# A hybrid pooling and windowed-attention layer on eight cores: another order of the loads and first projections in the opening

## The reference, cut to what matters

```python
# x (16, 4096, 1024), ctx (16, 256, 1024), one layer
shift, scale, gate = adaln(c, w_mod, b_mod)          # silu(c) @ w_mod + b_mod, three blocks of 1024
h_ctx = modulate(rms_norm(ctx, g_pre), c_shift, c_scale)
k_ctx, v_ctx = h_ctx @ w_in[:, K], h_ctx @ w_in[:, V]
h = modulate(rms_norm(x, g_pre), shift, scale)
xa, ga, q, k, v, gb, gm = split_columns(h @ w_in)    # 512, 512, 1024, 256, 256, 1024, 2048
y_a = pool_mixer(xa, pool_w, pool_scale) * silu(ga)
y_b = windowed_attention(rope(q), rope(k), v, k_ctx, v_ctx, sink) * silu(gb)
        # 16 heads, keys of block i-1, i, i+1 (128 each) and 256 context keys; exp(sink) joins the sum
g = sigmoid(gm)
merged = g[:, :1024] * (y_a @ w_branch_a) + g[:, 1024:] * (y_b @ w_branch_b)
out = x + gate * rms_norm(merged @ w_out, g_post)
```

## Time and profile before

| | us |
|---|---|
| median of 2 runs | 2343.43 (2341.91 to 2344.96) |
| the profiled execution | 2342.27 |
| its span on the slowest core (0) | 2340.7 |
| spans of the eight cores | 2330.9 to 2340.7 |
| PE busy, of the span | 2215.8 (95%) |
| first steady step starts at about | 262 |

### The profile page before, as it was taken

How to read it: one execution, slowest core, us unless ns; L and a number is a source line. 1 busy time by engine, 2 the same in 40 slices (tenths; PEclk the granted TensorE clock), 3 DMA queues, 4 the chain that set the end, 5 groups by cost and what they waited for, 6 DMA issues and landing times.

```text
span 2340.7 us, 50018 instructions; the slowest of 8 cores (2330.9 to 2340.7 us)
## 1 busy us (share of the span) xinstructions
PE 2215.8 (95%) x16101; PEld 1030.9 (44%) x16392; DVE 1281.3 (55%) x3176; ACT 1185.6 (51%) x2291; POOL 870.5 (37%) x1074
## 2 busy tenths in 40 slices
PE   7478899999999999999999999999999999999997
PEld 2234344444444444444444444444444444444443
DVE  1225556555565655556566645656565565656542
ACT  2235554546555455545545465555556555554531
POOL 1212434343342434334343433434343433434333
PEclk9779999999999999999999999999999999999999
DMA  8975855655555564645556475545546554544353
GB/s 233 246 99 92 154 153 154 166 146 155 164 137 147 157 166 134 164 150 142 149 162 177 140 172 163 138 141 153 161 140 163 162 149 137 162 136 145 100 184 127
DMA packets 209171, 358.12 MB, mean 153 GB/s; under 512 B 131884, under 2 KB 134060, under 8 KB 206520
## 3 DMA queue, kind: packets, MB, share of 16 engines
q1 hardware_dynamic: 206024, 335.97, 49.9%
q0 software_dynamic: 2896, 18.94, 5.9%
HBM read 310.09 MB, written 45.10 MB: 152 GB/s over the span
## 4 chain that ended last, share of the span: by engine, by line
PE 82%; DVE 6%; DMA 5%; issue 4%; ACT 1%; POOL 1%; SPq 0%; DVEq 0%; ACTq 0%; POOLq 0%
PE pb L589 35%; PE pb L968 9%; PE pb L720 9%; PE pb L890 8%; PE pb L781 7%; PE pb L807 6%; PE pb L881 4%; PE pb L645 2%; DVE s_yb L825 2%; DMA s_xt<-x 1%; DVE s_scr L606 1%; DMA s_ropet<-rope 1%; PE pb L356 1%; DMA s_ws<-wg_scr 1%; DVE s_Ga L713 1%
## 5 line engine op out<-in xcount | busy, mean ns | idle before, releaser
L784 ACT ACTIVATE s_PT<-pb 128x512 bf16<-128x512 f32 x1264 | 652.1, 605 | 214.0 <-PE pb L781 214.0
L589 PE MATMUL pb<-s_hT,s_ws 128*128 128x512 bf16 x2665 | 645.3, 382 | 13.8 <-DMA s_ws<-wg_scr 3.0
L589 PEld LDWEIGHTS pb<-s_hT,s_ws 128*128 128x128 bf16 x2784 | 262.0, 98 | 341.1 <-issue 52.9
L922 POOL TENSOR_TENSOR s_mgT<-s_scr 128x512 bf16<-128x512 f32 x128 | 163.4, 1277 | 585.7 <-DVE s_scr L861 580.2
L589 PE MATMUL pb<-s_hT,s_W 128*128 128x512 bf16 x1502 | 346.7, 382 | 3.7 <-issue 2.3
L861 DVE SCALAR_TENSOR_TENSOR s_scr<-s_Tm,pb 128x512 f32<-128x512 bf16 x256 | 175.4, 685 | 294.0 <-PE pb L890 121.2
L856 ACT ACTIVATE s_Tm<-pb 128x512 bf16<-128x512 f32 x256 | 154.8, 605 | 263.0 <-PE pb L589 211.7
L606 DVE TENSOR_TENSOR s_scr<-pb,s_ropet 128x512 f32<-128x512 f32 x320 | 204.1, 685 | 138.2 <-PE pb L589 91.8
L720 PE MATMUL pb<-s_W,s_hT 128*128 128x512 bf16 x1003 | 241.4, 381 | 1.3 <-issue 0.3
L968 PE MATMUL pb<-s_ws,s_mgT 128*128 128x512 bf16 x956 | 231.1, 381 | 6.7 <-DMA s_ws<-wg_scr 1.5
L589 PEld LDWEIGHTS pb<-s_hT,s_W 128*128 128x128 bf16 x1536 | 144.7, 98 | 197.2 <-issue 36.6
(11 more groups left out here) (138 smaller groups left out, 2239.5 us busy)
## 6 DMA issues: line engine op xcount, KB each, us to landing
s_ws<-wg_scr SPq DMA_DIRECT2D x344, 512.0 KB, 4.5
s_xr<-x SPq DMA_DIRECT2D x63, 512.0 KB, 4.7
y<-s_xr SPq DMA_DIRECT2D x60, 512.0 KB, 5.0
s_xt<-x SPq DMA_DIRECT2D x58, 512.0 KB, 4.7
wg_scr<-w_g POOLq DMA_DIRECT2D x22, 512.0 KB, 12.6
s_ropet<-rope SPq DMA_DIRECT2D x16, 512.0 KB, 4.5
s_ws<-w_mod SPq DMA_DIRECT2D x5, 1024.0 KB, 13.3
s_W<-w_in POOLq DMA_DIRECT2D x4, 1024.0 KB, 22.7
```

The source lines that it names most:

```text
L589: E("pe", lambda e, k=k, rhs=rhs: e.matmul(out=pb[:, :], lhsT=lhs(k), rhs=rhs, start=(k == 0), stop=(k == 7)), reads=hb + wbufs(k), writes ...
L784: E("act", lambda e, g=g: e.activation(out=PT[:, jb, g, :], in_=banks[g][0][:, :], func=AF.Exp, scale=0.125), reads=[banks[g][1]], writes= ...
L922: E("pool", lambda e: e.tensor_tensor(out=mgT[:, c, :], in0=u[0][:], in1=v[0][:], op=ALU.add), reads=[u[1], v[1]], writes=[bf(f"mgT{c}")])
```

## The change

It does six things. The six loads of ctx and x are issued without waiting for W2 and W3. The order behind them becomes rope, `w_mod` blocks 4 and 5, then `sink`, the next tile, the `g_rows`. Five of the 22 `gcast` are issued by POOL at once behind the weight casts, before the first projection, and the other 17 from 16.0 on at 3.6 (before: all 22 from 28.0 at 3.8); the first four `gload` go from 62 to 74. On PE the context's norms and transposes come before the values, only one of the four `q_unit` of group 0 stands before the woven part, `ctx_kv(0)` comes behind the transposes of tiles 4 to 7, then three `q_unit`, and `esink` (ACT), the values of group 1, `gate_rows(4)`, keys of group 1, `gate_rows(5)`; attention starts at 19.5 of the planned clock, not 12.5. In the later part of the opening the `xa`, `ga`, `ctx_kv(1)`, `q_unit` and pooling steps change places, and `pool_flush(3)` follows `pool_next(3)` at once. The PE transposes of tiles 0 to 3 are put out 4.5 later than their `pvs` and that of tile 63 3.0 later; `pvs` moves from 0.83 and 0.91 of a tile's width to 0.85 and 0.92 in every tile.

```diff
-                    later(3.0, P(turn_yb, t)) if 4 <= t < TT - 1 else turn_yb(t)
+                    later(3.0 if t >= 4 else 4.5, P(turn_yb, t))
-            ... (0.83, 1.2, P(pvs, 0)), (0.91, 1.2, P(pvs, 2))]
+            ... (0.85, 1.2, P(pvs, 0)), (0.92, 1.2, P(pvs, 2))]
...
-        for n in range(2):
-            next_load([bf("W2")])
-        ld(sinkb, sink_d.partition_broadcast(128), "sinkb", [bf("sinkb")])
+        for n in range(6):
+            next_load()
         load_rope(0)
-        for n in range(4):
-            next_load([bf("W3")])
         load_wmod(4)
         load_wmod(5)
+        ld(sinkb, sink_d.partition_broadcast(128), "sinkb", [bf("sinkb")])
+        if BPC > 1:
+            next_load()
         for j in range(2):
             ...grow loads
-        if BPC > 1:
-            next_load()
         ld(view(edge, 0, [[1, 64]]), edge_d, "edge", [bf("edge")])
         mod_quad(0, act=(1, 4, 7))
+        casts = list(range(14)) + [20, 14, 15, 16, 17, 21, 18, 19]
...
-        E("act", lambda e: e.activation(out=esink[:], in_=sinkb, func=AF.Exp), ...)
-        k_unit(0)
-        v_unit(0, 0)
-        v_unit(0, 1)
+        for i in range(5):
+            gcast(casts.pop(0))
         norm_sum()
         norm_sum()
         xs = [norm_scale(), norm_scale()]
-        q_unit(0, 0)
-        turn_pe_ctx(xs[0], 0, "dve")
-        q_unit(0, 1)
-        turn_pe_ctx(xs[1], 1, "act")
         norm_sum()
         norm_sum()
+        k_unit(0)
+        for j in range(2):
+            turn_pe_ctx(xs[j], j, "act")
+        xs = [norm_scale(), norm_scale()]
         mod_ctx()
-        xs = [norm_scale()]
-        q_unit(0, 2)
-        xs.append(norm_scale())
         norm_sum()
-        q_unit(0, 3)
         norm_sum()
-        load_rope(1)
-        xs.append(norm_scale())
-        xs.append(norm_scale())
+        v_unit(0, 0)
+        v_unit(0, 1)
+        xs += [norm_scale(), norm_scale()]
+        q_unit(0, 0)
...
+        first = [(0.45, P(front_turn, i, 4 + i, 0, ("dve", "act")[i % 2])) for i in range(4)]
+        if BPC > 1:
+            first += [z(next_load)]
+        first += [(3.5, P(ctx_kv, 0)), z(mod_quad, 1, range(8), (1, 4, 7))]
+        first += [(3.46, P(q_unit, 0, r)) for r in range(1, 4)] + [z(load_rope, 1), z(esink_exp)]
+        first += [(1.75, P(v_unit, 1, 0)), (1.75, P(v_unit, 1, 1)), (7.0, P(gate_rows, 4)), (3.46, P(k_unit, 1)), (7.0, P(gate_rows, 5)), z(load_gg, 0)]
...
+        first += [(1.73, P(ga_unit, 0, c)) for c in range(4)] + [z(pool_part, 0, 6.0)]
...
+        first += [(3.46, P(q_unit, 1, 3)), z(pool_next, 3, 5.0), z(pool_flush, 3)]
         first += [(1.73, P(ga_unit, 1, c)) for c in range(4)]
         for n, g in enumerate(casts):
-            later(28.0 + 3.8 * n, P(gcast, g))
+            later(16.0 + 3.6 * n, P(gcast, g))
         for n in range(2, NSL):
-            later(62.0 + 3.8 * n, P(gload, n))
-        run(first, range(4), 12.5)
+            later(74.0 + 3.8 * n, P(gload, n))
+        run(first, range(4), 19.5)
```

More of the change, by code:

```diff
@@ L1034, in pvs @@
                 if g0:
-                    later(3.0, P(turn_yb, t)) if 4 <= t < TT - 1 else turn_yb(t)
+                    later(3.0 if t >= 4 else 4.5, P(turn_yb, t))
             fr = [0.02, 0.18, 0.34, 0.50, 0.66] if nb == 5 else [0.02, 0.20, 0.40, 0.60]
             s = [(f, 0.75, P(vis, jb)) for jb, f in enumerate(fr)]
-            s += [(0.10, 1.73, P(gb, t, 0)), (0.26, 1.73, P(gb, t, 1)), (0.83, 1.2, P(pvs, 0)), (0.91, 1.2, P(pvs, 2))]
+            s += [(0.10, 1.73, P(gb, t, 0)), (0.26, 1.73, P(gb, t, 1)), (0.85, 1.2, P(pvs, 0)), (0.92, 1.2, P(pvs, 2))]
             s.sort(key=lambda v: v[0])
@@ L1217, in build_program @@
             cast(ws[:, i, :], wg_d[18 + i], [bf(f"ws{i}")])
-        E("act", lambda e: e.activation(out=esink[:], in_=sinkb, func=AF.Exp), reads=[bf("sinkb")], writes=[bf("esink")])
-        k_unit(0)
-        v_unit(0, 0)
-        v_unit(0, 1)
+        for i in range(5):
+            gcast(casts.pop(0))
         norm_sum()
@@ L1248, in front_turn, with esink_exp @@
             (turn_pe_ctx if ctx else turn_pe_lat)(xs[n], j, eng)
-        first = [(3.5, P(ctx_kv, 0))] + [(0.45, P(front_turn, i, 4 + i, 0, ("dve", "act")[i % 2])) for i in range(4)]
-        first += [z(mod_quad, 1, range(8), (1, 4, 7)), (3.46, P(k_unit, 1)), (1.75, P(v_unit, 1, 0)), (1.75, P(v_unit, 1, 1))]
+        def esink_exp():
+            E("act", lambda e: e.activation(out=esink[:], in_=sinkb, func=AF.Exp), reads=[bf("sinkb")], writes=[bf("esink")])
+        first = [(0.45, P(front_turn, i, 4 + i, 0, ("dve", "act")[i % 2])) for i in range(4)]
@@ L1252, in build_program @@
         if BPC > 1:
-            first += [z(next_load), z(front_norm), z(front_norm)]
-        first += [(7.0, P(gate_rows, 4))]
+            first += [z(next_load)]
+        first += [(3.5, P(ctx_kv, 0)), z(mod_quad, 1, range(8), (1, 4, 7))]
+        first += [(3.46, P(q_unit, 0, r)) for r in range(1, 4)] + [z(load_rope, 1), z(esink_exp)]
+        first += [(1.75, P(v_unit, 1, 0)), (1.75, P(v_unit, 1, 1)), (7.0, P(gate_rows, 4)), (3.46, P(k_unit, 1)), (7.0, P(gate_rows, 5)), z(load_gg, 0)]
+        first += [z(next_load)] if BPC == 1 else [z(front_norm), z(front_norm)]
@@ L1255, in build_program @@
+        first += [(0.25, P(fold_unit, k)) for k in range(8)]
+        first += [(1.73, P(xa_unit, 0, c)) for c in range(4)]
         if BPC > 1:
-            first += [(0.45, P(front_turn, 4 + j, j, 1, "act")) for j in range(2)] + [z(mod_ctx)]
-        first += [(7.0, P(gate_rows, 5)), z(load_gg, 0)]
+            first += [(0.45, P(front_turn, 4 + j, j, 1, "act")) for j in range(2)] + [z(mod_ctx), z(next_load)]
+        first += [(1.73, P(xa_unit, 1, c)) for c in range(4)]
+        first += [(1.73, P(ga_unit, 0, c)) for c in range(4)] + [z(pool_part, 0, 6.0)]
@@ L1258, in build_program @@
         if BPC > 1:
             first += [(3.5, P(ctx_kv, 1))]
[L1260 to L1265, removed]
@@ L1266, in build_program @@
-        first += [(3.46, P(q_unit, 1, 3)), z(pool_flush, 3)]
+        first += [(3.46, P(q_unit, 1, 0)), z(pool_next, 1, 6.0), (3.46, P(q_unit, 1, 1)), (3.46, P(q_unit, 1, 2)), z(pool_next, 2, 5.0)]
+        first += [(3.46, P(q_unit, 1, 3)), z(pool_next, 3, 5.0), z(pool_flush, 3)]
         first += [(1.73, P(ga_unit, 1, c)) for c in range(4)]
-        casts = list(range(14)) + [20, 14, 15, 16, 17, 21, 18, 19]
         for n, g in enumerate(casts):
-            later(28.0 + 3.8 * n, P(gcast, g))
+            later(16.0 + 3.6 * n, P(gcast, g))
```

## The result

The changed kernel takes 2378.4 us (median of two runs, 2377.3 and 2379.4) against 2343.4: 1.0149 times the time before [1.0105, 1.0193], 1.5% slower. The forecast was 2346 with a range up to 2364, so it was wrong: the change was forecast to cost next to nothing and costs 35 us. Some executions of every kernel here ran several per cent longer at a lower clock on one die or both; all ratios are of the others. The profiled run took 2377.3; its slowest core is core 5 (2375.8 us), where it was core 0 before (2340.7).

The account below looks back on a forecast made before the run. PE was busy 95% of the span; the opening's stretch was bound by a 512 KB load (rope) and an 8 KB one (sink). 2342.3 + 15 (sink stall) - 11 (later transposes, clock) = 2346.3, left at 2346; range 2316 to 2364.

Parts of the forecast that it names:

- Step (1), loads without waits: Opening: six tile loads fit the gap before the casts and beside the key weights; costs nothing, at worst 4 us.
- Step (2): Opening: rope issued about 55.3, ctx's norms freed, gate_rows(4) ending near 106, not 147.8; order wins about 40 us.
- Step (3), the sink: Opening: sink waits behind w_mod 4 and 5 and ten gcasts of 4.0 us; lands about 149 (138 or 157).
- small pieces travel together: Rival, 22%: eight 1 KB pieces count as one packet, sink passes before the gcasts, rope(1) is late; 2325 us.
- Step (4), from the sink to gate_rows(5): ACT waits for the sink, PE idles 107 to about 152, gate_rows(5) ends about 172; +15 us (+3 to +22).
- Steps (5) to (8), the second half: Later transposes, moved pvs, remaining gcasts with later gloads, and pool order; together -11 us.
- Nothing is given back: Rival, 21%: in the second half DVE, not the yb wait, limits PE, so the 11 us fall away; 2359 us.
- Steps (5) and (6): Later transposes of tiles 0 to 3: -9 us and -2 for clock (-13 to 0); moved pvs: 0 (-3 to +3).
- steps (7) and (8): Second half: twelve gcasts remaining with later gloads, 0; pool_flush(3) straight behind pool_next(3), 0, up to +4 us.
- The last transpose: Tile 63's later transpose: a wait of the same kind, 1 us, taken at nothing.
- No blockade: Rival, 7%: gcasts do not hold back the loads; gate_rows(5) ends near 125, 32 us early; 2299 us.
- The slower side: Rival, 21%: DVE limits PE in the second half and the 11 us fall away; 2359, or 2368 with 4.8 us gcasts.

Follow-up runs that it names:

- both: Changed kernel with sink, g_rows and edge loads issued ahead of rope and all gcasts back at the earlier kernel's times; ratio to before 0.9936 [0.9901, 0.9971].
- five gcasts alone: Kernel before, with only five gcasts issued straight behind the weight casts, the other 17 from 28.0 on; ratio to before 1.0068 [1.0039, 1.0097].
- loads alone: Kernel before, with only the six loads of ctx and x no longer waiting for W2 and W3; ratio to before 0.9921 [0.9891, 0.9950].
- no yb: Changed kernel with the transposes and pvs put back as before the change; two runs, 2381.6 and 2397.0 us.

## Why the prediction was wrong, step by step

The mechanism was the one forecast: a sink behind w_mod 5 and the gcasts, ACT standing for it, PE out of banks in vis(1). The direction and the class (within 2%, which I gave 94%) came out too; the size did not. On the slowest core 35.1 us were lost where I had 4, and the 31.1 between them lie in three places: 11.4 up to the end of gate_rows(5), 10.9 in the second half and 8.8 after it. In the mean of the cores, which the accident of one core moves less, it is 8.8, 16.2 and 1.4, and 4.6 for a slowest core further from the mean.

**Step (1), loads without waits: right.** The keys start at 58.45 behind hT's landing, 2.4 us later than the earlier trace rows; priced 0 to 4. Alone, the step is worth 13.8 us at gate_rows(5).

**Step (2): right.** DVE had rope by 69.09 (forecast 68.5), and PE ran until 100. But gate_rows(4), which I had put ahead of vis(1) and finished by about 107, stood behind it.

**Step (3), the sink: right in kind, 8.9 us short.** One packet of each queue in turn, also for pieces of 1 KB: 1018 to 1012 packets from 62 to 105 us, with 5.85 MB against 3.07, and 230 to 230 from 110 to 145. That refutes the rival *small pieces travel together*, and with it the rule of the Trainium skill ("DMA: Bandwidth & Descriptors", Queues, rings and completion order) of 9 to 17 descriptors a packet, as far as it goes for these loads. What was short is the price of a gcast. Ten of them went ahead of the sink, as forecast. Their 160 packets of 32 KB began at 98.7 us (I had 103) and were over at 153.2 (I had 145); the sink came 4.7 us behind them (I had 4). So ten gcasts took 54.5 us where I had 41.5: the packets alone 45.6, 4.56 a gcast and not 4.0, q1's packets between them 6.0 where I had 1.5, and 2.9 that I can't place. My upper bound of 157 used 4.8; the sink came at 157.9.

The 4.0 was a mean over two prices.'s own stretch in two parts, q0 of core 0 before the change, 130 to 150 us and 150 to 180:

```profile
q0 software_dynamic: 144, 2.62, 78.1%
q0 software_dynamic: 194, 3.15, 95.3%
```

That is 3.1 us a gcast and then 4.8, with 19 packets of q1 in all: it was not for want of the other queue that the first were cheap. In 130 to 140 four of the eight cores had gcasts in flight, from 150 on all eight, and after the change all eight from 102 on. That the gcasts of the other cores set the price fits the traces of five kernels (before, after, both, five gcasts alone, loads alone): some 3 us a packet where few cores copy or all copy with pauses, some 4.7 where all copy without a pause. No run tests it by an edit.

**Step (4), from the sink to gate_rows(5): forecast +15, measured +26.4** (183.7 on core 5 against 157.3) and 23.8 in the mean of the cores. Of the 11.4, 8.9 are the sink's. The other 2.5 (with 0.3 from rounding of my 172) are work: I let 23 us pass between the sink and the end, 15 of products, with margins for ACT and the clock; it was 25.8, as gate_rows(4) stood behind the stall with 9.55 us (7.38 before), while PE began 0.9 us behind the sink and not 3. (The margins that I named, 3 and 3, make 21 with the 15 of products; 2 us of my 23 have no term.)

**Steps (5) to (8), the second half: in the mean of the cores this is the term that failed by most.** Forecast -11, measured +5.2 (-0.1 on the slowest core). By its sum it is the case that I called *Nothing is given back*, at a higher price; by its parts it is not. Steps (5) and (6) held: the transposes with the moved `pvs` gave 8.2 us in the changed kernel (13.4 in the kernel before). What failed is what I put at nothing in steps (7) and (8), or did not price at all: the other order of the second half, with a first half that ends in a stall. It cost 13.4 (107.9 to 121.3, "no yb"), and 13.4 less 8.2 is the 5.2. Of the 13.4, 10.8 are idle time of PE (14.1 to 24.9) and 2.5 busy time, at a granted clock of 0.87 where it was 0.92. The idle time stands ahead of two lines: 8.5 us ahead of L807 (0.8 before) and 3.3 ahead of L428 (0.9 before). Groups of PE in the second half (busy us, mean ns | idle us before them, what ended it), of the changed kernel, core 5, 183.7 to 293.1:

```profile
L807 PE MATMUL pb<-s_Vr,s_PT 128*128 128x65 bf16 x176 | 11.2, 199 | 7.1 <-DVE s_PT L794 7.1
...
L428 PE MATMUL pb<-s_ya,s_mgT 128*128 128x128 bf16 x32 | 3.7, 249 | 6.1 <-DVE s_W L434 3.4 <-ACT s_PT L784 1.2 <-DVE s_yb L825 1.0
L845 PE MATMUL pb<-s_ident,s_yb 128*128 128x128 bf16 x24 | 3.6, 247 | 3.8 <-DVE s_yb L825 2.0 <-issue 1.3 <-DVE s_small L816 0.2
```

and of the kernel with the transposes and pvs alone, core 0, 156 to 250:

```profile
L807 PE MATMUL pb<-s_Vr,s_PT 128*128 128x65 bf16 x176 | 9.9, 193 | 0.0
...
L845 PE MATMUL pb<-s_ident,s_yb 128*128 128x128 bf16 x32 | 3.3, 218 | 0.8 <-DVE s_yb L825 0.7
L428 PE MATMUL pb<-s_ya,s_mgT 128*128 128x128 bf16 x32 | 2.6, 219 | 0.9 <-DVE s_Gb L723 0.9
```

The stretches are 109.4 and 94.0 us long (on the second core the half itself is 90.4), and PE is idle for 18.6 and 5.1 us of them: 7.1 more ahead of L807, 5.2 more ahead of L428, 3.0 more ahead of L845, 2.6 less ahead of L781.

*The fold (L428).* `ctx_kv(1)` stood ahead of it before the change and stands behind it now; that is a cover moved away which I did not price. Over all cores the wait is 5.8 to 6.4 us in the eight kernels with the new place and the later transposes, 3.3 to 3.5 in "no yb", which has the new place without them, and 0.4 to 0.9 in the five with the old. So the new place goes with some 2.5 us, and the rest comes only with the transposes beside it. No kernel moved `ctx_kv(1)` back alone; this is argued from traces and not shown by its own edit.

*The product with the masked probabilities (L807).* The wait is 3.6 to 11.5 us over all cores of the nine kernels with the new first half and 0 to 1.8 in the five with the old. Its longest piece, 6.9 us up to 284.7 on core 5, can be followed on DVE:

```profile
279.66 0.65 DVE L752 SCALAR_TENSOR_TENSOR s_sF<-s_sF,s_xa 128x128 f32<-128x128 f32 x1 [0.65 <-POOL s_sF L733]
...
282.05 0.29 DVE L752 SCALAR_TENSOR_TENSOR s_sF<-s_sF,s_xa 128x128 f32<-128x128 f32 x1 [0.55 <-POOL s_sF L733]
...
283.91 1.29 DVE L794 TENSOR_TENSOR s_PT<-s_PT,s_maskb 128x1024 bf16<-128x1024 bf16 x2
```

The mask (L794) stands in DVE's list behind the two pool steps, and inside PE's wait DVE itself waits 1.6 us for POOL's sums. That is the sign that I had named for this rival, DVE waiting for POOL while PE waits for DVE. But the old order of the pool, xa, ga and query steps brings the wait only from 7.1 to 4.7 in the mean (in "both" from 7.1 to 6.9): that order is not its main cause. Which of the edits that remain is (`lead` of 19.5 for 12.5, the later places of the context transposes and of `ctx_kv(1)`), stays open.

**The last transpose**, taken at nothing: at tile 63 PE waits 6.1 us for the attention result, where the longest such wait after the opening was 1.3 before. Each core has 4 to 6 us there. The changed kernel's waits of PE, core 5, from 300 us on:

```profile
PE pb L845 <- DVE s_yb L825: 6.1, 1, 6.1
```

**The rivals.** *No blockade* (2299) fell with the sink. *The slower side* came nearest: 2368 with gcasts of 4.8 us. I gave it 21% and let the range cut its upper part. As measured on the slowest core the sum is 2342.3 + 26.4 - 0.1 + 8.8 = 2377.4. The 8.8 lie in the rest of the span, which the forecast took as unchanged; 4.8 of them are the longer wait at tile 63.

**Where the gain went.** The gcasts' early issue costs 35.5 us at gate_rows(5), the sink and the g rows behind w_mod 19.9 more. Without these two the change is 0.6% faster than before (0.9936), and two lines of it alone are as good (0.9921).

## What to carry to other kernels

Before a load is moved behind others, ask what each engine does when it is the last to land: eight kilobytes behind 4 MB of weights held ACT for 72 us, and freeing ACT only showed the next small load in the same place. A copy from DRAM to DRAM that goes in large packets taxes every packet of the other queue with its whole length, so count packets and not bytes. Before a price is taken from a stretch, cut the stretch in two: a mean of 4.0 us hid prices of 3.1 and 4.8. When a term is forecast to be won in one stretch, look up what stood as cover ahead of each wait there, and test the parts alone: the two lines that paid were hidden in a change that lost.
